# The order in which ScalarE and VectorE split u tiles, v tiles and weights in the expert loop of a two-layer encoder

## The reference, cut to what matters

```python
u = peer_u[eb]                                              # rows of the picked experts
a = jax.nn.gelu(jnp.einsum('thkd,td->thk', u, xb).astype(jnp.float32))
wgt = (a * gb).astype(xb.dtype)                             # times the gate of each pick
return jnp.einsum('thk,thkd->td', wgt, peer_v[eb])
```

## Time and profile before

| | us |
|---|---|
| median of 3 runs | 5005.16 |
| lowest, highest | 5004.92, 5009.96 |
| the profiled execution, its own time | 5007.78 |
| its span in the profile | 5006.0 |
| TensorE busy (share of the span) | 4198.0 (84%) |
| VectorE busy | 3155.8 (63%) |
| ScalarE busy | 1736.2 (35%) |
| GpSimd busy | 1391.9 (28%) |
| mean granted clock of TensorE | 0.921 of full speed |

### The profile page before, as it was taken

One profiled execution on the slowest core, in us unless ns is written; L12 is line 12 of the kernel. 1 busy time (PEld: TensorE's weight loads), 2 busy tenths in 40 slices (PEclk: granted clock), 3 DMA queues, 4 the chain that ended last, 5 costly groups with the idle time before them and its releaser, 6 DMA issues. The chain is left out here.

```text
span 5006.0 us, 64200 instructions
## 1 busy us (share of the span) xinstructions
PE 4198.0 (84%) x21706; PEld 3734.1 (75%) x21706; DVE 3155.8 (63%) x5125; ACT 1736.2 (35%) x2506; POOL 1391.9 (28%) x992
## 2 busy tenths in 40 slices
PE   8869798646799999999897797886467999999997
PEld 6669677546688888888776796775466888888887
DVE  3464334599677777777735543336896777777776
ACT  2242222109543343333322322221094334334333
POOL 0143101155322322322201531112553232232231
PEclk9989899879899999999998898998798999999999
DMA  3100212105877777777531003120058777777775
GB/s 116 47 9 1 101 59 72 34 1 131 249 261 244 242 251 242 251 246 243 198 104 42 9 1 110 64 67 26 1 140 270 247 245 251 244 247 249 239 249 196
DMA packets 458568, 750.34 MB, mean 150 GB/s; under 512 B 241232, under 2 KB 278864, under 8 KB 458192
## 3 DMA queue, kind: packets, MB, share of 16 engines
q1 hardware_dynamic: 384720, 480.40, 29.5%
q0 software_dynamic: 73728, 268.47, 15.8%
HBM read 696.35 MB, written 52.43 MB: 150 GB/s over the span
## 5 line engine op out<-in xcount | busy, mean ns | idle before, releaser
L123 PE MATMUL banks<-act_hi,exp_uT_hi 128*128 128x384 f32 x2048 | 742.8, 363 | 183.6 <-DVE exp_uT_lo L1994 183.6
L1913 POOL DMA_INDIRECT exp_u_gathered<-in_peer_u,row_experts x256 | 390.3, 1525 | 1601.3 <-DVE exp_row_a L1999 1532.3
L124 PE MATMUL banks<-act_hi,exp_uT_lo 128*128 128x384 f32 x2048 | 732.7, 358 | 0.0
L125 PE MATMUL banks<-act_lo,exp_uT_hi 128*128 128x384 f32 x2048 | 732.4, 358 | 0.0
L124 PE MATMUL banks<-exp_v_hi,exp_w_lo 128*128 128x512 f32 x1536 | 598.4, 390 | 0.0
L123 PE MATMUL banks<-exp_v_hi,exp_w_hi 128*128 128x512 f32 x1536 | 598.1, 389 | 0.0
L125 PE MATMUL banks<-exp_v_lo,exp_w_hi 128*128 128x512 f32 x1536 | 597.7, 389 | 0.0
L123 PEld LDWEIGHTS banks<-act_hi,exp_uT_hi 128*128 128x128 f32 x2048 | 416.2, 203 | 208.1 <-DVE exp_uT_lo L1994 205.6
L124 PEld LDWEIGHTS banks<-act_hi,exp_uT_lo 128*128 128x128 f32 x2048 | 416.4, 203 | 2.4
L125 PEld LDWEIGHTS banks<-act_lo,exp_uT_hi 128*128 128x128 f32 x2048 | 415.2, 203 | 0.0
L1972 ACT CAST exp_v_hi<-exp_v_raw 128x1024 fp32r<-128x1024 f32 x256 | 268.0, 1047 | 355.1 <-PE banks L125 354.7
(11 more groups left out here) (386 smaller groups left out, 8295.8 us busy)
## 6 DMA issues: line engine op xcount, KB each, us to landing
exp_uT_raw<-in_peer_uT SPq DMA_DIRECT2D x260, 512.0 KB, 4.2
exp_v_raw<-in_peer_v SPq DMA_DIRECT2D x256, 512.0 KB, 4.3
exp_gates<-dense_gates SPq DMA_DIRECT2D x256, 192.0 KB, 2.7
win_project_raw<-in_w_in SPq DMA_DIRECT2D x32, 1024.0 KB, 5.5
dense_gates<-gate_block SPq DMA_DIRECT2D x6, 4096.0 KB, 20.7
wkv_project_raw<-in_w_xkv SPq DMA_DIRECT2D x16, 1024.0 KB, 5.0
wpq_project_raw<-in_peer_wq SPq DMA_DIRECT2D x16, 1024.0 KB, 5.1
dense_gates<-last_gates SPq DMA_DIRECT2D x4, 4096.0 KB, 20.7
```

What stands on the lines that cost most here:

```text
L123: pe.matmul(out, lhs[0], rhs[0], start=first, stop=False)
L124: pe.matmul(out, lhs[1], rhs[0], start=False, stop=False)
L125: return pe.matmul(out, lhs[0], rhs[1], start=False, stop=last)
L1913: pool.indirect_dma_start(out, None, table, bass.IndirectOffsetOnAxis(SL.row_idx[:, slot:slot + 1], 0)).then_inc(done, 16)
```

## The change

The instructions of the loop stay the same on every engine; ScalarE and VectorE get them in another order, and the waits move with them. In a group, ScalarE before: v_hi 0, gelu 0, w_hi 0, then for tiles 1 to 3 v_hi, u_hi of the next tile, gelu, w_hi, and last u_hi of tile 1 of the next group. Now: v_hi 0, then for `e` = 0 to 2 u_hi of tile `e + 2` (behind product `e`), gelu `e`, v_hi `e + 1`, w_hi `e`; then gelu 3, u_hi of tile 5 (tile 1 of the next group), w_hi 3. VectorE follows the same order with the low parts and the gates product. SyncE, GpSimd and TensorE are not touched.

```diff
             u_hi(0, 0)
             u_hi(1, 1)
+            def v_hi(g, e):
+                act.wait_ge(v_in[e % 2], g * 32 + (e // 2) * 16 + 16)
+                act.copy(vh[:, e], vr[:, e % 2]).then_inc(vho, 1)
+            def gelu(n, e):
+                act.wait_ge(am, n + 2)
+                act.wait_ge(wlo, n + 1)
+                act.activation(w[:, e % 2], PS[:, 2 + e % 2, 0:DTOK], ACT.Gelu_apprx_tanh).then_inc(ge, 1)
+            def w_hi(n, e):
+                act.wait_ge(wo, n + 3)
+                act.copy(wh[:, e], w[:, e % 2]).then_inc(who, 1)
             with act.Fori(0, NG) as g:
-                for e in range(GROUP):
-                    n = g * GROUP + e
-                    act.wait_ge(v_in[e % 2], g * 32 + (e // 2) * 16 + 16)
-                    if e == 0:
-                        act.wait_ge(om, g * NO + 1)
-                    act.copy(vh[:, e], vr[:, e % 2]).then_inc(vho, 1)
-                    if e:
-                        act.wait_ge(am, n + 1)
-                        u_hi(n + 1, (e + 1) % 2)
...
-                act.wait_ge(am, g * GROUP + GROUP + 1)
-                u_hi(g * GROUP + GROUP + 1, 1)
-                act.wait_ge(rd, g * GROUP + GROUP)
+                n = g * GROUP
+                act.wait_ge(om, g * NO + 1)
+                v_hi(g, 0)
+                for e in range(GROUP - 1):
+                    act.wait_ge(am, n + e + 2)
+                    u_hi(n + e + 2, e % 2)
+                    gelu(n + e, e)
+                    v_hi(g, e + 1)
+                    w_hi(n + e, e)
+                gelu(n + GROUP - 1, GROUP - 1)
+                u_hi(n + GROUP + 1, 1)
+                w_hi(n + GROUP - 1, GROUP - 1)
+                act.wait_ge(rd, n + GROUP)
                 act.activation(rg[:], ra[:], ACT.Gelu_apprx_tanh).then_inc(rge, 1)
...
             with dve.Fori(0, NG) as g:
+                n = g * GROUP
+                v_lo(n, 0)
+                for e in range(GROUP - 1):
+                    u_lo(n + e + 2, e % 2)
+                    gated(g, n + e, e)
+                    v_lo(n + e + 1, e + 1)
+                    w_lo(n + e, e)
+                gated(g, n + GROUP - 1, GROUP - 1)
+                u_lo(n + GROUP + 1, 1)
+                w_lo(n + GROUP - 1, GROUP - 1)
```

More of the change, by code:

```diff
@@ L1964, in _ @@
             u_hi(1, 1)
-            with act.Fori(0, NG) as g:
-                for e in range(GROUP):
-                    n = g * GROUP + e
-                    act.wait_ge(v_in[e % 2], g * 32 + (e // 2) * 16 + 16)
-                    if e == 0:
-                        act.wait_ge(om, g * NO + 1)
-                    act.copy(vh[:, e], vr[:, e % 2]).then_inc(vho, 1)
-                    if e:
-                        act.wait_ge(am, n + 1)
-                        u_hi(n + 1, (e + 1) % 2)
[L1976 to L1980, removed]
-                act.wait_ge(am, g * GROUP + GROUP + 1)
-                u_hi(g * GROUP + GROUP + 1, 1)
-                act.wait_ge(rd, g * GROUP + GROUP)
+            def v_hi(g, e):
[8 more added lines that the diff above has]
+                act.copy(wh[:, e], w[:, e % 2]).then_inc(who, 1)
+            with act.Fori(0, NG) as g:
+                n = g * GROUP
[11 more added lines that the diff above has]
+                act.wait_ge(rd, n + GROUP)
                 act.activation(rg[:], ra[:], ACT.Gelu_apprx_tanh).then_inc(rge, 1)
@@ L2017, in _, with v_lo, gated, w_lo @@
             u_lo(1, 1)
-            with dve.Fori(0, NG) as g:
-                for e in range(GROUP):
[L2020 to L2034, removed]
+            def v_lo(n, e):
+                dve.wait_ge(vho, n + 1)
+                dve.tensor_tensor(vl[:, e], vr[:, e % 2], vh[:, e].bitcast(F32), ALU.subtract).then_inc(vlo, 1)
+            def gated(g, n, e):
+                dve.wait_ge(ge, n + 3)
+                dve.wait_ge(g_in[e % 2], g * 32 + (e // 2) * 16 + 16)
+                dve.tensor_tensor(w[:, e % 2], w[:, e % 2], gt[:, e % 2], ALU.mult).then_inc(wo, 1)
+            def w_lo(n, e):
+                dve.wait_ge(who, n + 1)
+                dve.tensor_tensor(wl[:, e], w[:, e % 2], wh[:, e].bitcast(F32), ALU.subtract).then_inc(wlo, 1)
+            with dve.Fori(0, NG) as g:
+                n = g * GROUP
[8 more added lines that the diff above has]
+                w_lo(n + GROUP - 1, GROUP - 1)
+                for e in range(GROUP):
+                    row_product(g, e)
                 dve.wait_ge(rge, g + 1)
```

## The result

The changed kernel takes 5319.09 us (5309.34 to 5326.98, 4 runs) against 5005.52: a ratio of 1.0623, 95% interval 1.0604 to 1.0643, slower. Forecast were 5305 us, with a range of 5190 to 5400. The profiled span is 5307.5 us, 301.5 more than before; the sum had said 300.

A forecast was written before the change was run, and what follows sets the result against it. TensorE was taken to idle 2.28 us a group for u_lo 2; the change swaps this for chained load waits. +246 (settled groups) and +54 (first groups) on 5007.78 give 5307.8, median 2.6 lower: 5305 us, range 5190 to 5400.

The forecast's parts named there:

- the sum: Whole kernel: +246 us from 60 settled groups and +54 from first groups, +300 on the profiled 5007.78.
- Product 2's wait: TensorE's 2.28 us wait for u_lo 2 before product 2 of each group was to go, with 1.6 us to spare.
- The waits chain over SyncE's queue: Each tile's u load stands behind the previous tile's gates product in SyncE's queue, so each link waits for the one before.
- The link of 7.24 us: Per tile, gates product to load issue, landing (3.7), u_lo and next gates product: 7.24 us against 4.24 of product.
- The table load behind the cast: ScalarE: table load 1.06 us after u_hi 2's start, gelu 1.29 later, no drain; a drain would add 84 us.
- The sizes inside a group: Settled group: idle 6.7 us against 2.28, 40.0 at full clock, 41.3 with the dip, +4.1 on 37.22.
- the 1.4: Slower TensorE clock behind the last idle piece of a group: 1.4 us added, bounds 0 and 1.8.
- First groups: First two groups of each layer, with u loads of 6.2 us: about +15 and +12, +54 over two layers.
- The rival of the intended gain: Raw tiles ready in time, only product 2's wait and dip go: group 33.3, -250, 4755 us; 4%.
- Rival 3: Loads of u and v share the DMA engines, u takes 4.6: group 44.0, +6.8, 5470 us; 10%.

The follow-up runs named there:

- e1: Changed kernel with SyncE issuing the u load of tile n+4 once u_lo of n+2 is written, ahead of the gates product wait: 4752.2 us, ratio 0.9485.
- e3: Changed kernel with gelu ahead of u_hi on ScalarE and the gates product ahead of u_lo on VectorE, SyncE untouched: 4922.9 us, ratio 0.9830.
- e4: Changed kernel with w_hi 3 ahead of u_hi 5 on ScalarE and w_lo 3 ahead of u_lo 5 on VectorE: 5205.0 us, ratio 1.0385.
- e8: e4 with the four row products also put ahead of u_lo 5 on VectorE: 5036.0 us, ratio 1.0050.
- e5: Changed kernel with SyncE issuing the u load ahead of the gates load, behind the same wait for the gates product: 5146.0 us, ratio 1.0276.

## Why the prediction was right, point by point

- *Product 2's wait goes.* Right: u_hi 2 at 4.5 us, no wait at product 2 in settled groups.
- *The waits chain over SyncE's queue.* Right, and shown from four sides: cut at the load (e1), at the gelu (e3), at the end (e4 with e8), shortened (e5). e1 and e3 came in their ranges; e5 and e8 gained more than expected, e4 less. That the new order costs engine time by itself is ruled out by e1, in which it runs with no wait of TensorE. ScalarE's waits for raw tiles were to be 2 to 4 us, three in a group; in 29 groups there are 86, 3.8 us on average, the longest 5.0.
- *The link of 7.24 us.* Gates product 0 was forecast for 7.47 and came at 7.50. The two links in the group shown were 8.2 and 6.8; over the 29 groups they were 7.44 and 7.13 on average. The u loads 3, 4 and 5 took 3.8, 3.6 and 3.8 us there, where I took 3.7 (the 4.0 of the profile's page is the median of all 260, and contains the one load of a group that is not on the path). The Trainium skill's 3.2 us ("DMA: Bandwidth & Descriptors", "Anatomy of one DMA — SWDGE (gpsimd) path") would have given the sum 90 us lower. That formula is stated for DMAs that GpSimd issues, and these are issued by SyncE; the trace has 3.2 us for the shortest of the loads only.
- *The table load behind the cast.* Cast, table load and gelu start at 1693.65, 1694.73 and 1696.02, so 1.08 and 1.29 us apart, where I had 1.06 and 1.29. The drain that the Trainium skill adds ("ScalarE: Activation LUTs", "What ACT_TABLE_LOAD costs"), about 1.38 us, is not seen here either.
- *The sizes inside a group.* The path of the sum held nearly term by term. The output products of tile 3 were forecast for 29.80 and start on average at 30.02; from there to the next group 10.2 + 1.3 of clock = 11.5 were forecast, and it is 11.62. Split by kind it looks otherwise: idle time was to be 6.7 us and is 5.3, the slower clock was to cost 1.3, at most 1.8, and costs 41.64 - 33.32 - 5.26 = 3.1. The difference is one oversight that costs nothing. The clock can be low behind both waits, and I counted it behind the last one only. Product 3 so takes some 1.8 us longer (3.1 less the 1.3 behind the last wait). But the output products of tile 3 start when the chain of loads lets them, and the waits for w are shorter by nearly as much (3.1 instead of 4.55 together; the one for w 2 comes in 8 of 29 groups only). Only the low clock behind the last wait lengthens a group. Windows: behind the wait before product 3, behind the last wait in the same group, and behind the last wait in another:

```profile
1704.98:1708.57 3.59, 3.59 (x11) 3.59 (x12) 2.02 (x3) 0.53 (x2) 0.00 (x0) 0.52 0.53 184
1720.21:1730.55 10.34, 10.34 (x46) 8.56 (x47) 9.82 (x15) 0.20 (x1) 7.03 (x6) 1.00 0.58 196
1428.55:1440.51 11.96, 11.96 (x46) 9.76 (x47) 11.34 (x16) 0.21 (x1) 8.77 (x7) 0.86 0.59 176
```

  This last piece takes 10.3 to 10.4 us in 8 of the 29 groups, 11.7 to 12.0 in 17 and 12.9 to 13.0 in 4. On average it is 1.3 above the shortest, as forecast; that it came so close is partly luck, since I had read the 1.4 from a dip at another place.
- *First groups.* Forecast 66 and 50 us, measured 63.87 and 48.50 in layer one, 64.30 and 50.47 in layer two. The last group of a layer (38.2) I had counted like the others, though `ahead` drops the wait for gates product 2 there.
- *The rival of the intended gain* failed on the late issue of load 3, as said. e1 gives its time, 4752 against 4755 worked out. How much sooner the load has to go is not tested: e1 issues it in the group before, some 22 us sooner, and not the 4 that I named.
- *Crowding.* Rival 3 took 317 GB/s at a DMA share of 0.85 as full. It isn't: e1's second group moves 338 GB/s at a share of 1.03, with TensorE busy all the time, and the loads on the path took 3.6 to 3.8 us and not 4.6.

```profile
1334.23:1367.55 33.32, 33.32 (x170) 30.48 (x168) 26.86 (x36) 14.30 (x19) 10.73 (x9) 1.00 1.03 338
```

- *Left out.* v_hi 0 now starts 1.56 us into the group (1690.70) instead of 0.20 (1526.01), since its table load comes behind the wait for the output bank. It cost nothing here: u_lo 2, VectorE's next piece, starts at 5.60 in all 29 groups, with VectorE idle before it.

## What to carry to other kernels

Moving a consumer ahead does not help beyond the point where its input is issued: look up in the issuing queue what the load stands behind. Where that is a product of the same chain, each tile waits for the one before, and everything placed behind the consumer on an in-order engine joins the chain. Move the order and the issue of the load together: here the new order alone cost 6%, the early loads alone gave nothing, and both gave 5%.

## What I had not expected of the hardware

In e1 the dips of the clock are gone with the waits. There a settled group takes 33.32 us at a granted clock of 1.00, so of the 3.9 us that it gains on the kernel before, 2.3 were idle time and 1.6 the slower clock behind it. The DMA engines carried the higher rate at once: 276 GB/s at a share of 0.84 against 247 GB/s and 0.73, and hardly a wait for data came of it: ScalarE waits once 0.8 us for a u tile and once 0.3 us for a v tile in 29 groups.
